# A decoder layer in float32: where the weight slots and the moving tiles start within their partitions

## What is computed

```
h = rmsnorm(x)
[z | xBC | dt | q | f | i | g | gates] = h @ w_in
y = SSD branch (conv, SiLU, chunked scan, norm)          # 4096 wide
o = HGRN2 branch (gated recurrence, norm)                # 2048 wide
m = sigmoid(gate_a) * (y @ w_br_a) + sigmoid(gate_b) * (o @ w_br_b)
x = x + rmsnorm(m @ w_out)
x = x + rmsnorm(relu(rmsnorm(x) @ w_up)^2 @ w_down)       # hidden 8192
x = x + sigmoid(rmsnorm(x) @ w_ple_gate) * (p @ w_ple_proj)
```

## Time and profile before

| | |
|---|---|
| median of 3 runs | 2767.23 us (2765.77 to 2768.04) |
| the profiled execution, time | 2765.75 us |
| its span, first to last instruction | 2763.8 us |
| TensorE (PE) busy | 2699.0 us, 98% |
| VectorE (DVE) busy | 1786.9 us, 65% |
| ScalarE (ACT) busy | 1420.3 us, 51% |
| GpSimd (POOL) busy | 183.0 us, 7% |
| mean DMA rate | 175 GB/s |
| granted TensorE clock | 0.996 of full |

### The profile page before, as it was taken

One profiled execution on the slowest core, in us unless ns is written; L12 is line 12 of the kernel. 1 busy time (PEld: TensorE's weight loads), 2 busy tenths in 40 slices (PEclk: granted clock), 3 DMA queues, 4 the chain that ended last, 5 costly groups with the idle time before them and its releaser, 6 DMA issues.

```text
span 2763.8 us, 59417 instructions
## 1 busy us (share of the span) xinstructions
PE 2699.0 (98%) x22077; PEld 2629.1 (95%) x22077; DVE 1786.9 (65%) x3214; ACT 1420.3 (51%) x2285; POOL 183.0 (7%) x297
## 2 busy tenths in 40 slices
PE   6999999999999999999989999989999999999999
PEld 5999999999999999999989999989999999999989
DVE  7878788844478888888864444576543356654475
ACT  6666666643366556556643434454443344444363
POOL 0111111100011111111110000000000000000000
PEclk9999999999999999999999999999999999999999
DMA  4544554455566566666555556435554455555534
GB/s 171 176 161 161 163 175 159 165 176 176 177 204 204 202 210 198 213 200 206 192 168 183 171 173 205 167 117 177 167 168 167 167 167 165 166 170 163 167 131 161
DMA packets 135289, 484.22 MB, mean 175 GB/s; under 512 B 17248, under 2 KB 19696, under 8 KB 134080
## 3 DMA queue, kind: packets, MB, share of 16 engines
q1 hardware_dynamic: 114560, 410.88, 44.5%
q0 software_dynamic: 20672, 72.55, 8.3%
HBM read 449.58 MB, written 33.78 MB: 175 GB/s over the span
## 4 chain that ended last, share of the span: by engine, by line
PE 84%; DVE 9%; ACT 3%; issue 2%; DMA 1%; DVEq 0%; POOL 0%; ACTq 0%; POOLq 0%
PE acc L1665 25%; PE acc L1666 24%; PE acc L1667 24%; DVE w_lo L1024 2%; DVE ccv L1310 1%; ACT w_hi L508 1%; PE bank L1665 1%; PE bank L1666 1%; PE bank L1667 1%; PE bank L1846 1%; PE bank L1954 1%; PE bank L1778 1%; PE bank L1941 1%; PE bank L1863 0%; DVE x L1509 0%
## 5 line engine op out<-in xcount | busy, mean ns | idle before, releaser
L1024 DVE TENSOR_TENSOR w_lo<-raw,w_hi 128x1024 fp32r<-128x1024 f32 x772 | 937.5, 1223 | 600.7 <-ACT w_hi L508 596.2
L1665 PE MATMUL acc<-h_hi,w_hi 128*128 128x288 f32 x3872 | 1159.4, 299 | 13.0 <-DVE h_lo L1061 9.0
L1667 PE MATMUL acc<-h_hi,w_lo 128*128 128x288 f32 x3872 | 1142.8, 295 | 0.0
L1666 PE MATMUL acc<-h_lo,w_hi 128*128 128x288 f32 x3872 | 1140.5, 295 | 0.0
L508 ACT ACTIVATE w_hi<-raw 128x1024 fp32r<-128x1024 f32 x772 | 809.6, 1053 | 437.8 <-PE acc L1667 393.6
L1665 PEld LDWEIGHTS acc<-h_hi,w_hi 128*128 128x128 f32 x3872 | 728.5, 188 | 21.4 <-issue 7.4
L1666 PEld LDWEIGHTS acc<-h_lo,w_hi 128*128 128x128 f32 x3872 | 728.9, 188 | 2.9
L1667 PEld LDWEIGHTS acc<-h_hi,w_lo 128*128 128x128 f32 x3872 | 728.0, 188 | 0.0
L1665 PE MATMUL acc<-u_hi,w_hi 128*128 128x288 f32 x1024 | 303.4, 296 | 0.0
L1667 PE MATMUL acc<-u_hi,w_lo 128*128 128x288 f32 x1024 | 302.1, 295 | 0.0
L1666 PE MATMUL acc<-u_lo,w_hi 128*128 128x288 f32 x1024 | 301.4, 294 | 0.0
(11 more groups left out here) (411 smaller groups left out, 3544.8 us busy)
## 6 DMA issues: line engine op xcount, KB each, us to landing
raw<-in_w SPq DMA_DIRECT2D x772, 512.0 KB, 3.3
ht<-in_ht POOLq DMA_DIRECT2D x64, 256.0 KB, 4.2
out_ssm_s<-ht POOLq DMA_DIRECT2D x64, 256.0 KB, 4.0
cbc<-cum_d POOLq DMA_DIRECT2D x8, 1152.0 KB, 6.9
hs<-in_s POOLq DMA_DIRECT2D x16, 512.0 KB, 4.6
out_hg_s<-hsn POOLq DMA_DIRECT2D x16, 512.0 KB, 5.0
x_in<-in_x SPq DMA_DIRECT2D x4, 576.0 KB, 5.9
mixb<-bmb POOLq DMA_DIRECT2D x16, 144.0 KB, 2.0
```

The lines of the kernel that those rows point to most:

```text
L1024: V.tensor_tensor(w_lo[:, k], raw[:, k], w_hi[:, k].bitcast(F32), ALU.subtract).then_inc(lo_done, 1)
L1665: M.matmul(out, w_hi[:, k, i], hi[:, kt0 + i, ::-1], start=first and i == 0, stop=False)
L1666: M.matmul(out, w_hi[:, k, i], lo[:, kt0 + i, ::-1], start=False, stop=False)
L1667: op = M.matmul(out, w_lo[:, k, i], hi[:, kt0 + i, ::-1], start=False, stop=last and i == SK - 1)
```

## The change

Five edits, all of placement and order.

1. `SLOT_GAP = 8`: 8 floats, 32 bytes, between the slots of w_hi and of w_lo. Slot k now starts 32 k further modulo 512: 128, 160, 192, 224. `raw` keeps its slots. `w_lo` starts at 49792, again 128 modulo 512.
2. `aligned` is gone. `h_hi` follows `w_lo` directly, at 66272, which is 224 modulo 512. `phase` becomes 112192, which is 64 modulo 512, and `p_hi` goes to 224 modulo 512 with the constants. `m_hi` stays at 480.
3. u starts 16 bytes behind `phase`, at 80 modulo 512, and is still written and read in reverse.
4. y also starts at 80 modulo 512, and is now written by L801 and L1452 in the normal order and read upwards.
5. `multiply` no longer reverses by itself; the callers hand it `rev(h_hi)` and so on, except for y.

These byte numbers follow from the sizes in the code. No instruction is added or removed, no semaphore is touched. The diff, its core:

```diff
+SLOT_GAP = 8
...
-    def aligned(at):
-
-        return (at - 480 + 511) // 512 * 512 + 480
+    def shifted(t):
+
+        return t[:, 4:].rearrange("p (i n) -> p i n", n=T)
...
-    w_hi = sb("w_hi", [P, RING, SK, P], F32R)
-    w_lo = sb("w_lo", [P, RING, SK, P], F32R)
-
-    place[0] = aligned(place[0])
+    SLOT = SK * P + SLOT_GAP
+    w_at = place[0]
+    w_his = sb("w_hi", [P, RING * SLOT - SLOT_GAP], F32R)
+    place[0] = w_at + (RING * SLOT * 4 + 511) // 512 * 512
+    w_los = sb("w_lo", [P, RING * SLOT - SLOT_GAP], F32R)
+
+    def slots(t):
+
+        return [t[:, k * SLOT:k * SLOT + SK * P].rearrange("p (i n) -> p i n", i=SK) for k in range(RING)]
+
+    w_hi, w_lo = slots(w_his), slots(w_los)
...
-    phase = place[0] = aligned(place[0])
+    phase = place[0]
...
-    y_hi = sb("y_hi", [P, 2 * KT, T], F32R)
-    y_lo = sb("y_lo", [P, 2 * KT, T], F32R)
+    y_hi = shifted(sb("y_hi", [P, 2 * KT * T + 4], F32R))
+    place[0] = phase + y_bytes
+    y_lo = shifted(sb("y_lo", [P, 2 * KT * T + 4], F32R))
...
-    u_hi = nc.alloc_sbuf_tensor_at("u_hi", [P, FT, T], F32R, offset=phase)
-    u_lo = nc.alloc_sbuf_tensor_at("u_lo", [P, FT, T], F32R, offset=phase + y_bytes)
+    u_hi = shifted(nc.alloc_sbuf_tensor_at("u_hi", [P, FT * T + 4], F32R, offset=phase))
+    u_lo = shifted(nc.alloc_sbuf_tensor_at("u_lo", [P, FT * T + 4], F32R, offset=phase + y_bytes))
...
-            nc.scalar.activation(y_hi[:, 4 * c:4 * c + 4], y32[:, 4 * c:4 * c + 4, ::-1], ACT.Copy).then_inc(y_his, 1)
+            nc.scalar.activation(y_hi[:, 4 * c:4 * c + 4], y32[:, 4 * c:4 * c + 4], ACT.Copy).then_inc(y_his, 1)
...
-            V.tensor_tensor(y_lo[:, 4 * c:4 * c + 4], y32[:, 4 * c:4 * c + 4, ::-1],
+            V.tensor_tensor(y_lo[:, 4 * c:4 * c + 4], y32[:, 4 * c:4 * c + 4],
...
-                M.matmul(out, w_hi[:, k, i], hi[:, kt0 + i, ::-1], start=first and i == 0, stop=False)
-                M.matmul(out, w_hi[:, k, i], lo[:, kt0 + i, ::-1], start=False, stop=False)
-                op = M.matmul(out, w_lo[:, k, i], hi[:, kt0 + i, ::-1], start=False, stop=last and i == SK - 1)
+                M.matmul(out, w_hi[k][:, i], hi[:, kt0 + i], start=first and i == 0, stop=False)
+                M.matmul(out, w_hi[k][:, i], lo[:, kt0 + i], start=False, stop=False)
+                op = M.matmul(out, w_lo[k][:, i], hi[:, kt0 + i], start=False, stop=last and i == SK - 1)
...
-                    multiply(*slab(U_GB, GB_SLABS, 0, u), ps[0][:, 0:T], h_hi, h_lo, SK * u, u == 0, u == 1)
+                    multiply(*slab(U_GB, GB_SLABS, 0, u), ps[0][:, 0:T], rev(h_hi), rev(h_lo), SK * u, u == 0, u == 1)
...
-                        multiply(*slab(fu + 2 * FT, 8, i, 4 * j + s), ps[j][:, 0:T], u_hi, u_lo, SK * s,
+                        multiply(*slab(fu + 2 * FT, 8, i, 4 * j + s), ps[j][:, 0:T], rev(u_hi), rev(u_lo), SK * s,
```

More of the change, by code:

```diff
@@ L507, in split_hi @@
                 act.wait_ge(slab_used, m * RING + (k + 1 - RING))
-            nc.scalar.activation(w_hi[:, k], raw[:, k], ACT.Copy).then_inc(hi_done, 1)
+            nc.scalar.activation(w_hi[k], raw[:, k], ACT.Copy).then_inc(hi_done, 1)
         def ahead(first, per, it, s):
@@ L1023, in split_lo @@
             dve.wait_ge(hi_done, m * RING + (k + 1))
-            V.tensor_tensor(w_lo[:, k], raw[:, k], w_hi[:, k].bitcast(F32), ALU.subtract).then_inc(lo_done, 1)
+            V.tensor_tensor(w_lo[k], raw[:, k], w_hi[k].bitcast(F32), ALU.subtract).then_inc(lo_done, 1)
         def ahead(first, per, it, s):
@@ L1656, in _, with rev @@
         M = nc.tensor
+        def rev(t):
+            return t[:, :, ::-1]
         def multiply(m, k, out, hi, lo, kt0, first, last, chunks=None):
@@ L1680, in multiply_pair @@
                 for k, out in zip(slots, (banks[0][:, 0:T], banks[1][:, 0:T])):
-                    M.matmul(out, w_hi[:, k, i], h_hi[:, kt0 + i, ::-1], start=first and i == 0, stop=False)
-                    M.matmul(out, w_hi[:, k, i], h_lo[:, kt0 + i, ::-1], start=False, stop=False)
-                    op = M.matmul(out, w_lo[:, k, i], h_hi[:, kt0 + i, ::-1], start=False, stop=last and i == SK - 1)
+                    M.matmul(out, w_hi[k][:, i], h_hi[:, kt0 + i, ::-1], start=first and i == 0, stop=False)
+                    M.matmul(out, w_hi[k][:, i], h_lo[:, kt0 + i, ::-1], start=False, stop=False)
+                    op = M.matmul(out, w_lo[k][:, i], h_hi[:, kt0 + i, ::-1], start=False, stop=last and i == SK - 1)
                     if i == SK - 1:
@@ L1733, in nxt @@
                             free(T_GB + 1, 0)
-                        multiply(*slab(U_GB, GB_SLABS, 0, u), ps[1][:, 0:T], h_hi, h_lo, SK * (u - 2), u == 2, u == 3)
+                        multiply(*slab(U_GB, GB_SLABS, 0, u), ps[1][:, 0:T], rev(h_hi), rev(h_lo), SK * (u - 2), u == 2, u == 3)
                     return
@@ L1737, in nxt @@
                     free(T_HG + s // 2, it * HG_TILES)
-                multiply(*slab(U_HG, HG_SLABS, it, s), ps[s // 2 % 2][:, 0:T], h_hi, h_lo, SK * (s % 2),
+                multiply(*slab(U_HG, HG_SLABS, it, s), ps[s // 2 % 2][:, 0:T], rev(h_hi), rev(h_lo), SK * (s % 2),
                          s % 2 == 0, s % 2 == 1, (n_lo, 2) if first and s < 2 else None)
@@ L1819, in _ @@
                 pe.wait_ge(hg_olo, HEADS // 2 * (s + 1) if t == 0 else HEADS)
-                multiply(*slab(U_GB, GB_SLABS, 0, 4 + 2 * t + s), (b_diag, b_att)[t][:, 0:T], o_hi, o_lo, SK * s,
+                multiply(*slab(U_GB, GB_SLABS, 0, 4 + 2 * t + s), (b_diag, b_att)[t][:, 0:T], rev(o_hi), rev(o_lo), SK * s,
                          s == 0, s == 1)
@@ L1826, in branch_b @@
                     free(T_GB + s // 2, j * 2)
-                hi, lo = (h_hi, h_lo) if s < 2 else (o_hi, o_lo)
+                hi, lo = (rev(h_hi), rev(h_lo)) if s < 2 else (rev(o_hi), rev(o_lo))
                 multiply(*slab(U_GB, GB_SLABS, j, s), ps[s // 2][:, 0:T], hi, lo, SK * (s % 2), s % 2 == 0, s % 2 == 1)
@@ L1874, in early_gate @@
                         pe.wait_ge(sg_spe, GROUPS)
-                multiply(*slab(U_GA, 2 * GA_SLABS, 0, u), gate_bank[t][:, 0:T], h_hi, h_lo, SK * (u % 2),
+                multiply(*slab(U_GA, 2 * GA_SLABS, 0, u), gate_bank[t][:, 0:T], rev(h_hi), rev(h_lo), SK * (u % 2),
                          u % 2 == 0, u % 2 == 1)
@@ L1884, in ssd @@
                         free(T_SG + t, g * SG_TILES)
-                    multiply(*slab(U_SG, SG_SLABS, g, s), ps[t % 2][:, 0:T], h_hi, h_lo, SK * (s % 2),
+                    multiply(*slab(U_SG, SG_SLABS, g, s), ps[t % 2][:, 0:T], rev(h_hi), rev(h_lo), SK * (s % 2),
                              s % 2 == 0, s % 2 == 1)
@@ L1986, in branch_a @@
                     if s < 2:
-                        multiply(*at, ps[0][:, 0:T], h_hi, h_lo, SK * s, s == 0, s == 1)
+                        multiply(*at, ps[0][:, 0:T], rev(h_hi), rev(h_lo), SK * s, s == 0, s == 1)
                     else:
@@ L2000, in out_tiles @@
                         pe.wait_ge(ga_lo, SK * (s + 1))
-                    multiply(*slab(U_OUT, 4, i, 2 * j + s), ps[j][:, 0:T], m_hi, m_lo, SK * s, s == 0, s == 1)
+                    multiply(*slab(U_OUT, 4, i, 2 * j + s), ps[j][:, 0:T], rev(m_hi), rev(m_lo), SK * s, s == 0, s == 1)
         out_tiles(0, True)
@@ L2014, in first_pairs @@
             for s in range(4):
-                multiply(*slab(fu, 4, 1, s), bank[s // 2][:, 0:T], h_hi, h_lo, SK * (s % 2), s % 2 == 0, s % 2 == 1)
+                multiply(*slab(fu, 4, 1, s), bank[s // 2][:, 0:T], rev(h_hi), rev(h_lo), SK * (s % 2), s % 2 == 0, s % 2 == 1)
                 if s == 2:
@@ L2018, in first_pairs @@
             for s in range(4):
-                multiply(*slab(fu, 4, 2, s), bank[2 + s // 2][:, 0:T], h_hi, h_lo, SK * (s % 2), s % 2 == 0,
+                multiply(*slab(fu, 4, 2, s), bank[2 + s // 2][:, 0:T], rev(h_hi), rev(h_lo), SK * (s % 2), s % 2 == 0,
                          s % 2 == 1)
@@ L2028, in up @@
                     for s in range(2):
-                        multiply(*slab(fu, 4, i, 2 * j + s), ps[j][:, 0:T], h_hi, h_lo, SK * s, s == 0, s == 1)
+                        multiply(*slab(fu, 4, i, 2 * j + s), ps[j][:, 0:T], rev(h_hi), rev(h_lo), SK * s, s == 0, s == 1)
             if half == 0:
@@ L2064, in _ @@
                     w = 2 * j + i
-                    M.matmul(out, w_hi[:, k, w], p_hi[:, i, ::-1], start=i == 0, stop=False)
-                    M.matmul(out, w_hi[:, k, w], p_lo[:, i, ::-1], start=False, stop=False)
-                    op = M.matmul(out, w_lo[:, k, w], p_hi[:, i, ::-1], start=False, stop=i == 1)
+                    M.matmul(out, w_hi[k][:, w], p_hi[:, i, ::-1], start=i == 0, stop=False)
+                    M.matmul(out, w_hi[k][:, w], p_lo[:, i, ::-1], start=False, stop=False)
+                    op = M.matmul(out, w_lo[k][:, w], p_hi[:, i, ::-1], start=False, stop=i == 1)
                 op.then_inc(pj_tile if j < 3 else slab_used, 1)
@@ L2076, in ple @@
                 for s in range(2):
```

(2 more changed lines are left out.)

## The result

The changed kernel takes 2775.81 us (median of 5 runs, 2773.4 to 2777.11); the kernel before took 2767.01 us beside it (5 runs). The ratio is 1.0032, with an interval of 1.0019 to 1.0046. I had forecast 2749 us, a gain, within 2700 to 2795. The time lies in that range, but it moved the other way.

The account below looks back on a forecast made before the run. TensorE's matmul pace was taken to bound the kernel (18,528 matmuls at 131.7 ns, 88% of the span). A gain of 18.5 us less 1 gave 2748.2 us for the profiled execution, forecast 2749, range 2700 to 2795.

Parts of the forecast that it names:

- What bounds the kernel, and where the change can act: TensorE: 18,528 matmuls at 131.7 ns, 88% of the span; only the 11.7 ns over columns, 217 us, can pay.
- The period of 128 bytes: Moving tiles against weights: if place matters, its period is 128 bytes or a divisor, since tiles 128 i further keep pace.
- The value taken for an unseen relation: Matmuls at new starts against the weights: 1.0 ns gained each, from L1801, 1.4 ns under the present pace.
- The term of the sum: All 18,528 matmuls on TensorE gain 1.0 ns each, 18.5 us, less 1 us taken back.
- the present place is a good one: Three of four slots, and u and y, leave a good relation: 15,048 matmuls lose 1.4 ns, 21 us, 2788; chance 0.28.
- nothing happens: The 9.7 ns belong to streaming fp32r on TensorE in any layout: 2766 us, within 2761 to 2771; chance 0.20.
- the stall mostly goes: Other relations or 16-byte starts end half of the stall: 4.6 ns on 18,528 matmuls, 85 us, 2681; chance 0.12.

Follow-up runs that it names:

- the run with 256 columns: Kernel with only the slots' 32-byte gap, second and third matmul of each product streaming 256 of 288 columns: 2634.73 us in one run.
- the run at 64: Kernel before with h, o, y, u and p at 64 modulo 128 instead of 96, weights and m untouched, no gap: 2788.54 us, ratio 1.0083.

## Why the prediction was wrong

**What bounds the kernel, and where the change can act: right.** The pace of 18,528 matmuls, read from starts, is what moved, and only that. The cost of turning y, of the 16-byte starts on the writers and of the slots on L1024 was nil, as said.

**The period of 128 bytes: it held for means over a slab, at 32-byte steps, with w_hi and w_lo at one place.** The rows did not show it as I read them. Twelve matmuls are four tiles, which pass through all four starts modulo 512, so their mean could not tell one start from another. Taken product by product from the unrounded starts of the kernel before, u's tiles take 394, 394, 398 and 394 ns in turn, and m's 397, 395, 394 and 394: neighbouring tiles differ by up to 4 ns a product, and only the sum over four is one number. The runs with w_lo moved, with starts 4 bytes apart and with starts 16 bytes off show too that the period is not the whole law.

**The value taken for an unseen relation: wrong, and this is the step that failed.** The term of the sum was 18,528 matmuls times a gain of 1.0 ns; measured is a loss of 13.7 us over them, 0.74 ns each. I took the gain from L1801, because it was the nearest row. It had another column count, other partitions, another direction and was read with a grain of 10 ns. Dividing what it had over its columns by 512, I made 130.3 ns of it for 288 columns at 64. The runs give 133.33 ns at 64 downwards and 132.2 upwards. In place of the gain stand 131.67, 133.33, 131.88 and 133.12 ns at the four relations: the three that the change brings in are all slower than the one that it leaves.

Whether the division was the fault is open. Undivided, L1801 has 16.7 ns over, against 11.7 for the 288-column matmuls, and would have spoken for a loss as well as for a gain; the run with 256 columns doesn't decide which is right. Nor is the row a fixed price. The timeline of PE in the changed kernel, the same instruction, with its tile again at 64 against the weight tile beside it:

```profile
496.06 0.40 PE L1815 MATMUL bank<-hvbd,hk 96*128 96x512 f32 x1
496.30 0.30 PE L1679 MATMUL acc<-h_hi,w_hi 128*128 128x288 f32 x1
```

Unrounded, the median over the 16 heads is 231 ns before and 237 in the changed kernel.

**The rival "the present place is a good one" is what happened.** Its place (three of four slots, and u and y) and its mark (a period of four slabs) are as it put them; its mechanism, two reads that meet, is not shown. Its price was 1.4 ns on 15,048 matmuls, 21 us. Measured: 0.2 to 1.7 ns on three slots, a mean of 0.8 over four, and 0.5 to 0.6 ns on u and y; 13.2 us in all, of which 3.9 us came back as less idle time. I had allowed 1 us for that, and in the case of a gain. With 0.28 it was held too unlikely. The argument against it was L1801 at 64, and for 288 columns read downwards 64 is the worst of the four.

**The rival "nothing happens"** fell with the run at 64, 22 us. By it TensorE's two reads would have met no one's; the Trainium skill (SBUF — State Buffer, Who interferes with whom) says that TensorE waits on nobody. The runs show something for which that leaves no room: moving one of the two operands against the other changes the pace by up to 1.7 ns in 132, moving both together by nothing. **The rival "the stall mostly goes"** has nothing for it: the lowest mean of any slot and tile in any full-length run is 131.3 ns.

**Open.** That the two reads get in each other's way inside a partition is argued from the relation; no view shows it. Why the best relation changes with the direction, the length and w_lo's place, why with starts 16 bytes off one relation has several paces, and what the some 9.4 ns per matmul are (11.7 less the 2.3 of the float32 row) that no placement took away, is not settled. None of the kernels beats the one before, so there is no better version to run.

## What to carry to other kernels

When TensorE runs back to back, read its pace from the starts, slab by slab: a change of 1% in it hardly shows in the durations (m's first matmul went from 296 to 297 ns) and not in the busy share (98% both times), and a periodic pace points to the buffer that it goes with. But a mean over a whole period hides what happens within it: look at single products before you say that a place makes no difference. Give all slots of a ring the same start modulo 128 bytes against the operand that is read beside them, unless you have measured the other relations; one measured place is worth more than four unmeasured ones. And where a price is taken from a row of another length, direction and partitions, ask first what makes it carry over; if nothing does, it gives a bound and not a sign.

## What the runs showed of the hardware

- The pace of fp32r matmuls depends on the relation of their two operands' addresses. Means over a slab, for 288 columns read downwards, with w_hi and w_lo alike modulo 512: 131.67, 133.33, 131.88 and 133.12 ns at 96, 64, 32 and 0 modulo 128; upwards 132.0, 132.2, 133.2 and 132.9. Moving both operands by 32 bytes leaves 131.7.
- Within a slab single products of three matmuls take 392 to 402 ns, in a pattern that repeats after two or four tiles in most slots (394, 394, 398 and 394 for u before).
- Starts 4 bytes apart can differ by 1.1 ns (131.7 at 96, 132.8 at 92).
- With starts 16 bytes off a multiple of 32, relation and direction do not fix the pace: upwards at 112, 131.3, 132.2 and 132.7 ns in three kernels.
- Of an fp32r matmul with 288 columns 11.7 ns are over the columns' time, of a float32 record 2.3. Whether the excess grows with the columns is not settled: 35 ns a product with 288, 288 and 288 columns and 37 with 288, 256 and 256 in slot 0, but 37.5 and 34.8 over the four slots.
- The writes here by ScalarE and VectorE are as fast from a reversed source as from a straight one (y: 1152 against 1150 and 1350 against 1350 ns), and as fast to a start 16 bytes off a multiple of 32 (u: 458 against 458 ns on VectorE).
